# Two thirds of the modulation vector as row sums on VectorE in a two-block transformer kernel

## The reference

```python
mod = jax.nn.silu(c) @ w_ada[i] + b_ada[i]
sh_a, sc_a, gt_a, sh_m, sc_m, gt_m = jnp.split(mod[:, None, :], 6, axis=-1)
mod_c = jax.nn.silu(c_ctx) @ w_ada[i] + b_ada[i]
csh_a, csc_a, cgt_a, csh_m, csc_m, cgt_m = jnp.split(mod_c, 6, axis=-1)
hc = modulate(rmsnorm(xc, norm1_g[i]), csh_a, csc_a)
s_f, s_b = context_states(hc, w_in[i], w_decay[i], b_decay[i])
h = modulate(rmsnorm(x, norm1_g[i]), sh_a, sc_a)
out, _, _ = token_mixer(h, w_in[i], w_decay[i], b_decay[i], gla_norm_g[i], w_pool[i],
                        pool_scale[i], w_out[i], s_f, s_b, rows)
x = x + (gt_a * out).astype(x.dtype)
h2 = modulate(rmsnorm(x, norm2_g[i]), sh_m, sc_m)
x = x + (gt_m * hier_moe(h2, ...)).astype(x.dtype)
```

## Time and profile before

| | |
|---|---|
| runs | 1242.98, 1242.77, 1241.24 us, median 1242.77 |
| profiled execution | 1242.8 us, its span 1241.0 us |
| PE, DVE, ACT busy | 93%, 54%, 40% of the span |
| chain that ended last | PE 84%, DVE 8%, ACT 4%, issue 2%, DMA 1% |
| read from memory | 256.05 MB, 207 GB/s over the span |
| mean granted clock of PE | 0.957 of full speed |

### The profile page before, as it was taken

The page is one execution under the profiler, slowest core; times in us unless marked ns, Lnnn a source line. Parts: engine busy times, 40 slices in busy tenths (PEclk is TensorE's granted clock), DMA queues, the critical chain, the costliest instruction groups (busy, mean ns, idle before and its releaser), DMA issues.

```text
span 1241.0 us, 19644 instructions
## 1 busy us (share of the span) xinstructions
PE 1153.9 (93%) x8302; PEld 971.2 (78%) x8302; DVE 670.2 (54%) x1045; ACT 499.2 (40%) x759; POOL 0.2 (0%) x4
## 2 busy tenths in 40 slices
PE   4889999799999997889999999799999999999986
PEld 2678868645555554789999987699889999999985
DVE  1646245513333335467655686857755676555576
ACT  2672323311111113444443543245874454443453
POOL 0000000000000000000000000000000000000000
PEclk8998979899999999999999979899999999999988
DMA  9713527799999967073555432233334646445320
GB/s 374 288 68 140 233 75 289 309 422 420 421 421 420 420 239 302 2 271 138 213 189 204 154 102 103 93 106 134 110 112 165 234 140 234 172 169 204 131 74 35
DMA packets 38156, 258.42 MB, mean 208 GB/s; under 512 B 4368, under 2 KB 5136, under 8 KB 7856
## 3 DMA queue, kind: packets, MB, share of 16 engines
q1 hardware_dynamic: 36720, 252.90, 53.0%
q10 hardware_dynamic: 1344, 4.21, 0.9%
HBM read 256.05 MB, written 1.05 MB: 207 GB/s over the span
## 4 chain that ended last, share of the span: by engine, by line
PE 84%; DVE 8%; ACT 4%; issue 2%; DMA 1%; ACTq 0%; DVEq 0%
PE bank L527 83%; DVE wl L1705 1%; ACT wh L1192 1%; DMA xt<-in_x 1%; DVE acc L1751 1%; DVE rstd L1729 1%; DVE arena L1900 1%; DVE xt L1742 0%; PE bank L887 0%; ACT arena L1202 0%; DVE hl L1756 0%; DVE arena L2249 0%; ACT L1202 0%; DVE small L2248 0%; PE bank L845 0%
## 5 line engine op out<-in xcount | busy, mean ns | idle before, releaser
L527 PE MATMUL bank<-hh,wh 128*128 128x256 f32 (+1 forms) x1256 | 366.7, 292 | 10.1 <-DVE hl L1756 6.2
L527 PE MATMUL bank<-hl,wh 128*128 128x256 f32 (+1 forms) x1256 | 360.8, 287 | 0.0
L527 PE MATMUL bank<-hh,wl 128*128 128x256 f32 (+1 forms) x1256 | 360.8, 287 | 0.0
L1705 DVE TENSOR_TENSOR wl<-raw,wh 128x1024 fp32r<-128x1024 f32 (+2 forms) x244 | 275.6, 1168 | 110.4 <-ACT wh L1192 109.3
L1192 ACT ACTIVATE wh<-raw 128x1024 fp32r<-128x1024 f32 (+2 forms) x244 | 234.4, 1005 | 93.0 <-PE bank L527 77.9
L527 PEld LDWEIGHTS bank<-hh,wh 128*128 128x128 f32 x1256 | 244.1, 194 | 16.7 <-issue 13.8
L527 PEld LDWEIGHTS bank<-hl,wh 128*128 128x128 f32 x1256 | 244.1, 194 | 2.1 <-issue 0.8
L527 PEld LDWEIGHTS bank<-hh,wl 128*128 128x128 f32 x1256 | 243.7, 194 | 1.1
L527 PE MATMUL bank<-yh,wh 128*128 128x256 f32 x512 | 146.7, 286 | 6.0 <-DVE yl L1725 3.7
L527 PE MATMUL bank<-yl,wh 128*128 128x256 f32 x512 | 146.2, 286 | 0.0
L527 PE MATMUL bank<-yh,wl 128*128 128x256 f32 x512 | 146.1, 285 | 0.0
(11 more groups left out here) (239 smaller groups left out, 1358.7 us busy)
## 6 DMA issues: line engine op xcount, KB each, us to landing
raw<-in_gu SPq DMA_DIRECT2D x40, 1024.0 KB, 15.3
arena<-in_gu SPq DMA_DIRECT2D x24, 1024.0 KB, 14.1
raw<-in_gd SPq DMA_DIRECT2D x22, 1024.0 KB, 13.3
raw<-in_w_ada SPq DMA_DIRECT2D x18, 1024.0 KB, 7.3
raw<-in_f1g SPq DMA_DIRECT2D x11, 1024.0 KB, 5.4
raw<-in_f2g SPq DMA_DIRECT2D x11, 1024.0 KB, 4.8
raw<-in_f2u SPq DMA_DIRECT2D x11, 1024.0 KB, 4.9
raw<-in_f2d SPq DMA_DIRECT2D x11, 1024.0 KB, 4.9
```

The costliest lines, as they stand in the source:

```text
L527: return pe.matmul(o, l, m, start=start, stop=stop, skip_group_check=True)
L1705: v.tensor_tensor(WL[slot_of[U]][:, 0:n], src, WH[slot_of[U]][:, 0:n].bitcast(f32), ALU.subtract).then_inc(S("wl"), 1)
```

## The change

Steps 0 to 3 stay as they are. The other 4096 outputs of the vector are laid with outputs on the partitions: the new array w_adt has 16 chunks [128, 2 x 1024], where each row holds the 1024 weights of one output. silu(c) is spread once: PE multiplies eight broadcast columns of CV by the identity, DVE copies the two banks into a new tile CB [128, 1024] that holds silu(c) in every partition. `dots(c)` on DVE then takes, for either half of chunk c, one scalar_tensor_tensor of 128x1024 (weights times CB) with accum_out, whose sum over the row is the output; the bias is added in `mod_rest`. PE's ada_rows(4) to (11) and turn(4) to (11) and ACT's copies for them go away. The chunks keep their places in the list and their buffers; they are given back by dots.

```diff
+        CB = sb("cb", [128, 1024])
...
         def add_ada(*pairs):
             for i in pairs:
-                add("w_ada", 2 * i)
-                add("w_ada", 2 * i + 1)
+                n, c = ("w_ada", 2 * i) if i < 4 else ("w_adt", 2 * i - 8)
+                add(n, c)
+                add(n, c + 1)
...
-        eaten = list(range(len(chunks)))
+        dotted = {where["w_adt", i]: i for i in range(16)}
+        eaten, at = [], 0
+        for c in range(len(chunks)):
+            eaten.append(at)
+            at += c not in dotted
...
-            if U in split_no:
+            if c in dotted:
+                e.wait_ge(*nth("dots", 2 * dotted[c] + 2))
+            elif U in split_no:
...
+        fixed((("cb", 0), 6), (("cb", 1), 7))
...
+            pe.wait_ge(*nth("d_p", 32))
+            for x in range(2):
+                b = take(pe, ("cb", x))
+                for k in range(4):
+                    t = mm(b[:, k * 128:k * 128 + 128], CV[:, 4 * x + k, 0:1].broadcast_to([128, 128]), ident, k == 0, True)
+                t.then_inc(S("cb"), 1)
             ada_rows(0)
...
-            ada_rows(4)
             lin_tm(("w1v", 1), [take(pe, ("v", 1, 0)), take(pe, ("v", 1, 1))], 4, HW, LW)
...
-            ada_rows(5)
-            turn(4)
...
-            turn(5)
...
-            ada_rows(6)
             outs(0)
...
-            turn(6)
...
-            ada_rows(7)
             states(3)
             scores(3)
-            turn(7)
...
-            ada_rows(8)
             outs(3)
-            turn(8)
...
-            ada_rows(9)
...
-            turn(9)
...
-            ada_rows(10)
             b = take(pe, "router")
...
-            ada_rows(11)
             b = take(pe, "rank")
...
-            turn(10)
-            turn(11)
...
+            def dots(*cs):
+                for c in cs:
+                    r = where["w_adt", c]
+                    arrived(v, r)
+                    for m in range(2):
+                        w = RAW[raw_of[r]][:, m * 1024:m * 1024 + 1024]
+                        v.scalar_tensor_tensor(w, w, 1.0, CB[:, :], ALU.mult, ALU.mult, accum_out=MOD3[:, 16 + 2 * c + m, 0:1]).then_inc(S("dots"), 1)
+
+            def mod_rest(lo, hi):
+                v.wait_ge(*nth("dots", hi - 16))
+                step(v.tensor_tensor(MOD3[:, lo:hi, 0], MOD3[:, lo:hi, 0], par("bada")[:, lo:hi], ALU.add))
+                prev()
...
+            for x in range(2):
+                v.wait_ge(*nth("cb", x + 1))
+                v.tensor_copy(CB[:, 512 * x:512 * x + 512], bank(("cb", x))[:, :]).then_inc(copied(("cb", x)), 1)
+                evicted(v, ("cb", x))
...
             through("w1v", 1)
             decay_apply(3)
+            dots(0, 1)
             given_back(v, first_in[EARLY_L])
...
+            dots(2, 3)
             through("w1g", 0)
...
             states(0)
             scores(0)
+            dots(4)
             through("w1g", 1)
             states(2)
             scores(1)
+            dots(5, 6)
             states(1)
             scores(2)
+            dots(7, 8)
             through("w_op", 0)
             states(3)
             scores(3)
+            dots(9)
+            head_gate(0)
             through("w_op", 1)
-            head_gate(0)
+            dots(10, 11)
             head_gate(1)
             through("w_og", 0)
             through("w_og", 1)
 
-            mod_rows(1, 16, 40, 10)
+            mod_rest(16, 40)
...
-            mod_rows(2, 40, 48, 12)
-            step(v.tensor_copy(G3, GTM))
...
                     if p % 2 == 0 and p < 14:
                         hot(q + 1)
+                    if p == 0:
+                        dots(12, 13, 14, 15)
+                        gate_mlp()
                     if p % 2 and p < 15:
                         gathered(q + 1)
...
-                        done(sp, "w_ada", 23)
+                        done(sp, "w_ada", 7)
...
-    A["w_ada"] = even(I["w_ada"][0], 0, 6144)
+    A["w_ada"] = even(I["w_ada"][0], 0, 2048)
+    A["w_adt"] = np.ascontiguousarray(I["w_ada"][0][:, 2048:].reshape(1024, 16, 2, 128).transpose(1, 3, 2, 0).reshape(16, 128, 2048))
```

More of the change, by code:

```diff
@@ L23 @@
 eps v_step a_step
-sc cv_zero turn mod1 mod2 hc_h hc_l tnc a_mm wo_mm
+sc cb cv_zero turn dots mod1 mod2 hc_h hc_l tnc a_mm wo_mm
 pool poolw yp_h yp_l dec la cu dexp dsec kt
@@ L246, in add @@
             where[name, i] = len(chunks)
-            chunks.append((a[i], a.shape[2], name not in ("w_ada", "w_r", "gu", "gd")))
+            chunks.append((a[i], a.shape[2], name not in ("w_ada", "w_adt", "w_r", "gu", "gd")))
         def add_ada(*pairs):
             for i in pairs:
-                add("w_ada", 2 * i)
-                add("w_ada", 2 * i + 1)
+                n, c = ("w_ada", 2 * i) if i < 4 else ("w_adt", 2 * i - 8)
+                add(n, c)
+                add(n, c + 1)
         add_ada(0, 1, 2)
@@ L403, in program @@
         st_jobs(2)
-        put(("scr", 1), ("ada", 6), ("o", 0), ("g", 1))
+        put(("scr", 1), ("o", 0), ("g", 1))
         st_jobs(1)
-        put(("scr", 2), ("o", 1), ("ada", 7))
+        put(("scr", 2), ("o", 1))
         st_jobs(3)
-        put(("scr", 3), ("o", 2), ("gn", 0), ("ada", 8), ("o", 3))
-        put(("wo", 0), ("wo", 1), ("gn", 1), ("ada", 9), ("wo", 2), ("wo", 3), ("wo", 4))
+        put(("scr", 3), ("o", 2), ("gn", 0), ("o", 3))
+        put(("wo", 0), ("wo", 1), ("gn", 1), ("wo", 2), ("wo", 3), ("wo", 4))
         job(("wo", 5), jobs["gn", 1][1])
         job("w_stat", 3)
-        put(("ada", 10), "router", *[("tm", a, q) for a in range(2) for q in range(2)])
-        put(("ada", 11), "rank")
-        job(("mod", 2), 3)
+        put("router", *[("tm", a, q) for a in range(2) for q in range(2)])
+        put("rank")
         rot = over([5, 6, 7], "g_")
@@ L579, in turn @@
             def turn(i):
-                if i in (0, 4, 10):
-                    take(pe, ("mod", {0: 0, 4: 1, 10: 2}[i]))
                 if i == 0:
+                    take(pe, ("mod", 0))
                     pe.wait_ge(*nth("d_p", 32))
@@ L980, in tensor_program @@
             pe.wait_ge(*nth("tm_h", 4))
-            evicted(pe, ("mod", 2))
+            evicted(pe, "w_stat")
             pe.wait_ge(*nth("flag", 1))
@@ L1361, in scalar_program @@
             head_out(1)
-            ada_row(7)
             through("w_op", 1)
@@ L1365, in scalar_program @@
             head_out(2)
-            ada_row(8)
             head_out(3)
@@ L1730, in root, with mod_first @@
                 prev()
[L1732 to L1736, removed]
+            def mod_first():
+                v.wait_ge(*nth("turn", 4))
+                src = BK[3][:, 0:32].rearrange("p (n c) -> p n c", c=2)
+                v.tensor_tensor(MOD3[:, 0:16, :], src, BA[:, 0:16, :].broadcast_to([128, 16, 2]), ALU.add).then_inc(copied(("mod", 0)), 1)
+                evicted(v, ("mod", 0))
+            def dots(*cs):
[9 more added lines that the diff above has]
+                prev()
             def add_out(i, name, scale):
@@ L1788, in vector_program @@
             v.wait_ge(*nth("d_p", 32))
-            mod_rows(0, 0, 16, 4)
+            mod_first()
             for c in range(2):
@@ L2037, in vector_program, with gate_mlp @@
             v.wait_ge(*nth("g32", 2))
+            def gate_mlp():
+                mod_rest(40, 48)
+                step(v.tensor_copy(G3, GTM))
+                prev()
             def grouped():
@@ L2118, in vector_program @@
                 grouped()
-            after, at[0] = at[0], before
+            after, at[0], stepped, own[1] = at[0], before, own[1], kept
             with v.Else():
                 dense()
-            assert at[0] == after and own[1] == kept
+            assert at[0] == after and own[1] == stepped
             v.nop().then_inc(S("moe"), 1)
```

8 lines of the change are left out of this document (1 added, 7 removed).

## The result

The changed kernel takes 1261.1 us (median of four runs: 1262.93, 1260.31, 1257.51, 1261.89), the kernel before 1242.03 in the same comparison: ratio 1.015, 95% interval 1.0125 to 1.0175, slower by about 19 us. The prediction was 1253.1 us, in a range of 1245 to 1264. The profiled execution, the slowest of the four, took 1262.93 us; its span is 1260.7, 19.7 more than before.

A forecast was written before the change was run, and what follows sets the result against it. Three regimes: the head, PE and DVE handing work over until about 241 us, then experts set by PE, 3% over DMA. Terms 0 + 2.9 - 2.6 - 1.2 - 0.8 + 12.0 = +10.3 on 1242.8: 1253.1 us, range 1245 to 1264.

The forecast's parts named there:

- rival D: PE, 100 to 240 us: gaps between short bursts keep it at 1.2 GHz for longer; 1258 to 1263 us; chance 6%.
- Price of a row sum: Each of the 32 new DVE instructions takes 1.2 us, 2.4 a chunk; bounds 1.15 and 1.3.
- Rival A: DVE: row sums run at half speed, 2.3 us each, 4.6 a chunk; +30 us, 1273 in total; chance 12%.
- Head: Start of the kernel: later constants offset by PE no longer idling before the row products; 0 us (-2.4 to +1.5).
- First hand-over: Pooling to states(0): DVE's four row sums delay the scaling and w1v 1, less removed PE work; +2.9 us.
- Second hand-over: states(0) to outs(2): removed PE work saves 7.0 us, but DVE is late, so only part counts; -2.6 us.
- up to the statistics: outs(2) to w_og: head norms come earlier by 2.6 us, less 1.4 for PE's slow start; -1.2 us.
- Rank: Between transposes and rank products: removing ada_rows(11) shortens DVE's wait for the rank; at most 0.96, taken -0.8 us.
- Expert stage: Late row sums hold buffers of gu 5 to 7 and gd 0, SP stalls, PE waits until up(3); +12.0 us (11 to 14).

The follow-up runs named there:

- filler work: Changed kernel plus 16 PE products on resident constants at each of the eight places of the removed projections, rows copied by ScalarE; 1255.38 us, ratio 1.0077 to 1.013.
- kernel with eight fillers: Changed kernel with all sixteen chunks' row sums in DVE's idle stretches, plus PE products on constants at all eight removed projections; 1228.76 us, ratio 0.9859 to 0.9914.

## Why the prediction was right, and where not

Sign and range were right, the size was 19 where +10.3 was forecast. The forecast's own bounds end near 1260 (1253.1, with 1.5 for the head, 3 for the hand-overs and 2 for the experts); that 1261.1 lies in the range is owed to rival D, which was let into it. By its own steps:

- **Price of a row sum**, 1.2 us in bounds of 1.15 to 1.3: 1.22, one every 1.145 us, 2.29 a chunk. Rival A is refuted: 2.3 us would show in every row of L1733. The Trainium skill, "Vector Engine (DVE) Microarchitecture Reference", section "Points that are easy to get wrong", has this instruction at half throughput with two non-bf16 sources in SBUF, as the prediction weighed. This case's trace does not agree: 1219 ns against 1222 for the subtraction of the same size; the measurement decides.
- **Head, 0**: the constants were there at 11.98 (12.1 expected), the row products from 18.73, 1.1 late, for 4.74 instead of 6.37. PE reached poolw at 106.36 instead of 107.00. Right, both halves of it.
- **First hand-over, +2.9**: +2.2. Scalings at 114.09 and 116.33, w1v 1 at 117.30 (118.0 expected). Right. (5.1 less 1.9 and 0.5 is 2.7, not 2.9.)
- **Second hand-over, -2.6, and up to the statistics, -1.2**: this is the step that failed. outs(2) was to start at 172.8 and w_og at 204.4; they started at 176.51 and 210.44. I let PE run "with the step lengths of before", charged a slow start only where it had stood for long, and took the order of waits from that. But outs(0) ran for 6.44 us, not 4.08, the gate products behind it were slow until 158, outs(3) took 6.98 instead of 4.08, and the router 7.01 instead of 5.08. So states(1) reached DVE at 162.38, when by the forecast it and scores(2) were to be done (162.4); they ended at 166.5, and dots(7, 8) and the split of w_op 0 followed, as foreseen, 4.1 late. Rival D was this mechanism, with 6% and as a case of its own; it was no rival but a term, and it held beside the forecast. With filler work outs(0) took 4.08 us again, the router's products 5.53, and the first up came 7.9 us earlier. The addition has a slip of its own: w_og 2.6 early less 1.4 is -1.2 against the kernel before, and +2.9 - 2.6 had already brought +0.3 of it, so the term was -1.5 and the sum +10.0.
- **Rank, -0.8**: the flag came at 242.22 instead of 236.55, 5.7 late after 3.4 at the statistics; the router's slow products alone are 1.9 of the difference. The gain was not to be seen.
- **Expert stage, +12.0**: the mechanism as described, gu 5 landing 4.84 us after its issue, up(1) waiting 7.40 us, up(3)'s second half last. It took 14.6, over the upper bound of 14. Chunks behind gu 5 came every (304.68 - 267.94) / 14 = 2.62 us, not 2.49, which is 1.9 of the 2.6 that were missing. The row sums didn't hold them: the 0.81 and 309 GB/s of 260 to 280 take in the stretch up to 263.1 in which nothing moved, and from 268 on the share is 1.00 or more, at 363 to 426 GB/s in stretches of 4 us and 422 behind 280. Why the late chunks landed slower than at 421 GB/s stays open.

-1.7 was the forecast for all ahead of the experts and +4.4 came. Of the 9.4 us that the sum lacked against the trace (19.7 for 10.3), 6.1 are there, 2.6 in the expert stage, 0.7 behind it.

## What to carry to other kernels

Moving work to an engine with idle time moves the release of its input buffers too: find on the new engine when they are given back, and what an in-order DMA issuer holds up behind them. That cost three quarters here, and putting the same instructions in stretches that the timeline shows idle, ahead of the wait and not behind it, gave the whole loss back by the median (1242.97 us). Work taken off TensorE at places where it waits anyway won nothing here and cost clock behind them: price the steps that follow it at both levels before you count the gain.

## What the hardware showed that I had not expected

PE's clock went down for steps that had not changed, once less work stood between them: outs(0), 24 records, took 4.08 us at 2.4 GHz (granted 1.00) and 6.44 mostly at 1.2 GHz (0.50 from 149 on), and 16 products on constants ahead of it, 1.9 us, brought it back. The kernel with eight fillers has nearly as many PE records as the kernel before (8286 and 8302) but 1141.3 us of busy PE instead of 1153.9, and ran 1.1% faster; some 6 us of the 14 are clock in a part of the program that was the same.

A scalar_tensor_tensor with two fp32 SBUF sources and accum_out runs at the pace of the plain subtraction of the same size (1219 against 1222 ns), its read-out of 0.09 us in the shadow of the next.
